# Normalising most of x in a transposed layout, with row statistics spread over the partitions through DRAM

## The reference, cut to what matters

```
hn   = x * rsqrt(mean(x*x, axis=-1) + 1e-6) * norm_g          # per token
proj = hn @ w_in                                              # 9216 columns
q, k, v, z_a, hc, gb, gc, z_b, g = split(proj)
attn = three dilated sliding-window groups, 8 heads of 64, merged by log-sum-exp
a    = (silu(z_a) * attn) @ w_attn_out
u    = gc * hc ;  conv = cw0*u[t-1] + cw1*u[t] + cw2*u[t+1]
c    = (silu(z_b) * gb * conv) @ w_conv_out
y    = rmsnorm(x + (sigmoid(g_a)*a + sigmoid(g_c)*c) @ w_o, final_g)
```

## Time and profile before

| | |
|---|---|
| median of 3 runs | 1518.55 us (1517.28 to 1518.56) |
| the profiled execution | 1517.51 us |
| its span on core 7 | 1515.9 us (cores: 1511.9 to 1515.9) |
| mean granted TensorE clock | 0.997 to 0.999 of full speed on every core |
| busy on core 7 | TensorE 1477.8, VectorE 927.4, ScalarE 697.8, GpSimd 141.5 us |
| moved by DMA | 132.07 MB, mean 87 GB/s |

### The profile page before, as it was taken

How to read it: one execution, slowest core, us unless ns; L and a number is a source line. 1 busy time by engine, 2 the same in 40 slices (tenths; PEclk the granted TensorE clock), 3 DMA queues, 4 the chain that set the end, 5 groups by cost and what they waited for, 6 DMA issues and landing times.

```text
span 1515.9 us, 28477 instructions; the slowest of 8 cores (1511.9 to 1515.9 us)
## 1 busy us (share of the span) xinstructions
PE 1477.8 (97%) x11360; PEld 848.1 (56%) x11360; DVE 927.4 (61%) x1477; ACT 697.8 (46%) x1169; POOL 141.5 (9%) x286
## 2 busy tenths in 40 slices
PE   4999999999999999999999999999999999999997
PEld 2454445577666666666766665766444444444443
DVE  4677777335775848667459575686854444445445
ACT  4445454344565656645356557565322222232222
POOL 4121113000010000100000000001100000000001
PEclk9999999999999999999999999999999999999999
DMA  9965554413150431502424205144943233343233
GB/s 250 153 127 102 117 103 81 72 39 83 32 104 15 100 54 38 82 14 45 106 38 94 40 17 112 27 95 67 188 103 108 83 105 91 84 111 105 62 112 125
DMA packets 67764, 132.07 MB, mean 87 GB/s; under 512 B 8752, under 2 KB 34480, under 8 KB 67376
## 3 DMA queue, kind: packets, MB, share of 16 engines
q1 hardware_dynamic: 49296, 96.70, 24.0%
q0 software_dynamic: 18336, 33.56, 16.5%
HBM read 130.17 MB, written 33.62 MB: 108 GB/s over the span
## 4 chain that ended last, share of the span: by engine, by line
PE 90%; DMA 6%; DVE 3%; issue 1%; ACT 0%; SPq 0%; POOL 0%; DVEq 0%; POOLq 0%; ACTq 0%
PE ps L405 52%; PE ps L699 10%; PE ps L1089 7%; PE ps L1119 6%; PE ps L855 6%; PE ps L719 3%; PE ps L808 3%; DMA X<-xw 2%; DMA gc_s<-X 2%; DMA X<-gc_s 2%; PE ps L450 1%; DVE X L905 1%; DMA v_s<-X 1%; DVE X L830 0%; DVE X L442 0%
## 5 line engine op out<-in xcount | busy, mean ns | idle before, releaser
L405 PE MATMUL ps<-hnT,wbf 128*128 128x512 bf16 (+1 forms) x3008 | 665.5, 373 | 2.6 <-DVE hnT L398 1.6
L405 PEld LDWEIGHTS ps<-hnT,wbf 128*128 128x128 bf16 x3008 | 282.1, 98 | 312.5 <-DVE X L894 2.6
L395 ACT ACTIVATE X<-ps 128x512 bf16<-128x512 f32 (+2 forms) x320 | 219.1, 693 | 201.7 <-PE ps L405 157.7
L820 ACT ACTIVATE X<-ps 128x512 bf16<-128x512 f32 x384 | 204.1, 614 | 116.9 <-PE ps L808 116.9
L405 PE MATMUL ps<-hnT,X 128*128 128x512 bf16 (+1 forms) x1152 | 245.5, 367 | 0.0
L870 DVE TENSOR_TENSOR X<-ps,X 128x512 f32<-128x512 f32 x128 | 110.9, 866 | 157.9 <-PE ps L855 118.5
L405 PEld LDWEIGHTS ps<-hnT,X 128*128 128x128 bf16 x1152 | 108.0, 98 | 125.2
L1094 DVE SCALAR_TENSOR_TENSOR hnT<-hnT,ps 128x512 f32<-128x512 f32 x128 | 87.1, 685 | 146.1 <-PE ps L1089 146.1
L830 DVE TENSOR_TENSOR X<-X,et 128x512 bf16<-128x512 bf16 x384 | 145.9, 419 | 37.3 <-ACT X L820 36.3
L699 PE MATMUL ps<-wbf,hnT 128*128 128x128 bf16 x2720 | 164.6, 220 | 0.0
L699 PEld LDWEIGHTS ps<-wbf,hnT 128*128 128x128 bf16 x2720 | 159.2, 114 | 3.3
(11 more groups left out here) (60 smaller groups left out, 982.4 us busy)
## 6 DMA issues: line engine op xcount, KB each, us to landing
X<-xw SPq DMA_DIRECT2D x80, 512.0 KB, 6.3
wbf<-w_in POOLq DMA_DIRECT2D x95, 256.0 KB, 6.0
y<-X SPq DMA_DIRECT2D x31, 512.0 KB, 3.9
X<-w_in POOLq DMA_DIRECT2D x17, 256.0 KB, 18.9
ga_s<-X SPq DMA_DIRECT2D x32, 128.0 KB, 4.2
X<-ga_s SPq DMA_DIRECT2D x8, 512.0 KB, 8.4
X<-gc_s SPq DMA_DIRECT2D x8, 512.0 KB, 9.1
gc_s<-X SPq DMA_DIRECT2D x24, 128.0 KB, 6.5
```

Source lines behind the costliest of these rows:

```text
L395: return op("act", lambda e: e.activation(out=out, in_=in_, func=AF.Copy), reads=reads, writes=writes)
L405: fns.append(lambda e, kt=kt: e.matmul(bv.cols(c0, n), lhsT=wf(kt), rhs=hnT.cols(kt * WT + t0, n), start=(kt == 0), stop=(kt == 7)))
L820: op("act", lambda e, bv=bank(sb_ + hh), hh=hh: e.activation(out=prv.cols(hh * 512, 512), in_=bv.cols(0, 512), func=AF.Exp, scale=0.125), ...
```

## The change

The host lays x down a second time, as `xt`: per 512 tokens (a group G) four blocks, each with 128 channels on the rows and, in a row, 512 tokens of one channel block and 512 of the next. The first nine tiles are handled as before. The other 39 are handled as ten groups of four tiles (one of three). For a group the kernel still loads its row-wise tiles and takes their squares and scales, but writes the scales as columns of a small tile `rs`, stores these to DRAM (`rs_s`), reads them back so that every partition holds all 512, and lets VectorE multiply the transposed loads by g (now one number per partition) and by those scales, straight into `hnT`. Stages N, T and E are gone for these tiles. `p1_until` now also runs in the middle of each step.

```
+        rs_d = nc.dram_tensor("rs_s", [10, 512], F32)
+        rb_ = [xb(75136 + 2048 * i, 2048, F32) for i in range(2)]
...
-        order = [8, 9, 10, 11, 7] + list(range(12, 41)) + list(range(0, 7)) + list(range(41, 48))
+        order = [8, 9, 10, 11, 7, 12, 13, 14, 15]
...
+        def xa_next():
+            k = xring["i"] % 6
+            xring["i"] += 1
+            return xa[k], "d_xa%d" % k
+
+        def group_events(k, G, nt):
+            t0, n, p = 0.3 + 2.8 * k, 128 * nt, k % 2
+            rb = rb_[p]
+            for t in range(nt):
...
+                def load(t=t, st=st):
+                    st["b"], sname = xa_next()
+                    dma("sp", sname, st["b"].v.base, bass.AP(xw, (512 * G + 128 * t) * D, [[D, 128], [1, D]]),
+                        writes=st["b"].r)
+
+                def square(t=t, st=st):
+                    rms_stat(st["b"].v.base, st["b"].r, xn_[2], out=(rs4.cols(4 * p + t, 1), R_rs4[p]))
+                at = t0 + (0.0, 0.3, 0.9, 1.2)[t]
+                p1ev.append((at, load))
+                p1ev.append((at + 1.0, square))
+
+            def store():
+                dma("sp", "d_rs%d" % p, bass.AP(rs_d, 512 * k, [[nt, 128], [1, nt]]), rs4.cols(4 * p, nt),
+                    reads=[R_rs4[p]], writes=[R_rsd[k]])
+
+            def spread():
+                dma("sp", "d_rb%d" % p, rb.v.cols(0, n), bass.AP(rs_d, 512 * k, [[0, 128], [1, n]]),
+                    reads=[R_rsd[k]], writes=rb.r)
+            p1ev.append((t0 + 2.25, store))
+            p1ev.append((t0 + 2.55, spread))
+            for q in range(4):
...
+                def load(q=q, st=st):
+                    st["b"], sname = xa_next()
+                    dma("sp", sname, st["b"].v.base, bass.AP(xt_d, (4 * G + q) * 128 * 1024, [[1024, 128], [1, 1024]]),
+                        writes=st["b"].r)
+
+                def norm(q=q, st=st):
+                    for j in range(2):
+                        op("dve", lambda e, j=j: e.scalar_tensor_tensor(
+                            out=hnT.ap((2 * q + j) * WT + 512 * G, [[128, nt], [1, 128]]),
+                            in0=st["b"].v.ap(512 * j, [[128, nt], [1, 128]]),
+                            scalar=cf.cols(CF_G + 2 * q + j, 1), in1=rb.v.ap(0, [[1, nt], [nt, 128]]), op0=ALU.mult, op1=ALU.mult),
+                           reads=st["b"].r + rb.r + [R_const], writes=hres(512 * G, 512 * G + n))
+                p1ev.append((t0 + 2.0 + 0.45 * q, load))
+                p1ev.append((t0 + 3.5 + 0.45 * q, norm))
+
+        for k, (G, nt) in enumerate(((4, 4), (5, 4), (6, 4), (7, 4), (8, 4), (9, 4), (10, 4), (1, 3), (0, 4), (11, 4))):
+            group_events(k, G, nt)
+        p1ev.sort(key=lambda x: x[0])
...
-                    conv_step(ct, c)
+                    conv_step(ct, c, mid=lambda: p1_until(stepi + 0.5))
                     stepi += 1
-                    p1_until(21.5 + (stepi - 8) * 1.3)
+                    p1_until(stepi)
                     stores.pop(0)()
```

More of the change, by code:

```diff
@@ L192, in build_program @@
     xw = nc.dram_tensor("xw", [XROWS, D], F32, kind="ExternalInput")
+    xt_d = nc.dram_tensor("xt", [XROWS // 512, 4, 128, 1024], F32, kind="ExternalInput")
     w_in = nc.dram_tensor("w_in", [INW, D], F32, kind="ExternalInput")
@@ L198, in build_program @@
     fgvec = nc.dram_tensor("fgvec", [128, D], F32, kind="ExternalInput")
-    cfp_d = nc.dram_tensor("cfp", [128, 32], F32, kind="ExternalInput")
+    cfp_d = nc.dram_tensor("cfp", [128, 40], F32, kind="ExternalInput")
     cbf_d = nc.dram_tensor("cbf", [128, 256], BF16, kind="ExternalInput")
@@ L223, in build_program @@
         stat_t = sb("stat", [128, 32], F32)
+        rs_t = sb("rs", [128, 8], F32)
         cbf_t = sb("cbfs", [128, 256], BF16)
@@ L228, in build_program @@
         dma_sem_names = (["d_w%d" % i for i in range(NWS)] + ["d_cw%d" % i for i in range(8)]
-                         + ["d_e0", "d_e1", "d_c", "d_c2", "d_gb", "d_fg", "d_wao", "d_wco", "d_g31", "d_vs20", "d_vs21"]
+                         + ["d_e0", "d_e1", "d_c", "d_c2", "d_gb", "d_fg", "d_wao", "d_wco", "d_g31", "d_vs20", "d_vs21", "d_rs0", "d_rs1", "d_rb0", "d_rb1"]
                          + ["d_xa%d" % i for i in range(6)] + ["d_x3%d" % i for i in range(6)] + ["d_y%d" % i for i in range(6)]
@@ L276, in build_program @@
         R_patt = Res()
+        rs4 = View(rs_t[:])
+        R_rs4 = [Res(), Res()]
+        R_rsd = [Res() for _ in range(10)]
         R_gad = [[Res() for _ in range(8)] for _ in range(4)]
@@ L333, in mrg @@
             return hnT.cols(dt_ * WT + m * 512, 512)
-        CF_HB, CF_CW, CF_FL, CF_BG, CF_MH = 0, 16, 28, 32, 48
+        CF_HB, CF_CW, CF_FL, CF_BG, CF_G, CF_MH = 0, 16, 28, 32, 48, 56
         def load_consts():
@@ L341, in load_consts @@
             dma("sp", "d_gb", gb_.v.base, bass.AP(gvec, 0, [[D, 128], [1, D]]), writes=R_gb)
-            dma("sp", "d_c2", cf.cols(CF_CW, 32), cfp_d.ap(), writes=[R_const])
+            dma("sp", "d_c2", cf.cols(CF_CW, 40), cfp_d.ap(), writes=[R_const])
             op("dve", lambda e: e.tensor_scalar(out=cf.cols(CF_HB, 16), in0=cf.cols(CF_BG, 16), scalar1=0.5,
@@ L409, in build_program, with rms_stat @@
         stat_ctr = {"i": 0}
-        def rms_stat(src, src_res, junk=junk_, eng="pool"):
+        def rms_stat(src, src_res, junk=junk_, eng="pool", out=None):
             k = stat_ctr["i"] % 8
@@ L420, in rms_stat @@
                                                  scalar2=EPS, op0=ALU.mult, op1=ALU.add), reads=[r], writes=[r])
-            op(eng, lambda e: e.tensor_tensor(out=stat.cols(c0 + 2, 1), in0=stat.cols(c0 + 1, 1),
-                                                 in1=cf.cols(CF_MH, 1), op=ALU.pow), reads=[r, R_mh], writes=[r])
-            return stat.cols(c0 + 2, 1), r
+            dst, dres = out if out is not None else (stat.cols(c0 + 2, 1), r)
+            op(eng, lambda e: e.tensor_tensor(out=dst, in0=stat.cols(c0 + 1, 1),
+                                                 in1=cf.cols(CF_MH, 1), op=ALU.pow), reads=[r, R_mh], writes=[dres])
+            return dst, dres
         R_gb = gb_.r
@@ L471, in build_program @@
-        p1ev.sort(key=lambda x: x[:3])
+        first = [[fn for (_, _, fn) in p1_stages(i, ti)] for i, ti in enumerate(order)]
+        xring = {"i": len(order)}
+        def xa_next():
[6 more added lines that the diff above has]
+            for t in range(nt):
+                st = {}
+                def load(t=t, st=st):
[16 more added lines that the diff above has]
+            for q in range(4):
+                st = {}
+                def load(q=q, st=st):
[11 more added lines that the diff above has]
+                p1ev.append((t0 + 3.5 + 0.45 * q, norm))
@@ L475, in p1_until @@
             while p1pos["i"] < len(p1ev) and p1ev[p1pos["i"]][0] <= t:
-                p1ev[p1pos["i"]][3]()
+                p1ev[p1pos["i"]][1]()
                 p1pos["i"] += 1
@@ L1299 @@
     cbf = np.ascontiguousarray(np.concatenate([_CACHE["pat"], _CACHE["idn"]], axis=1))
+    gcol = np.asarray(norm_g, np.float32)[0].reshape(8, 128).T
     in_maps = []
@@ L1311 @@
             flags[:, 3] = -1.0
-        cfp = np.ascontiguousarray(np.concatenate([cw, flags, bg], axis=1).astype(np.float32))
-        in_maps.append({"xw": xwin, "w_in": w_in2, "w_ao": w_ao, "w_co": w_co, "w_o": w_o2, "gvec": gvec,
+        cfp = np.ascontiguousarray(np.concatenate([cw, flags, bg, gcol], axis=1).astype(np.float32))
+        xt = np.ascontiguousarray(xwin.reshape(XROWS // 512, 512, 4, 2, 128).transpose(0, 2, 4, 3, 1)).reshape(
+            XROWS // 512, 4, 128, 1024)
+        in_maps.append({"xw": xwin, "xt": xt, "w_in": w_in2, "w_ao": w_ao, "w_co": w_co, "w_o": w_o2, "gvec": gvec,
                         "fgvec": fgvec, "cfp": cfp, "cbf": cbf, "etab": _CACHE["etab"]})
```

## The result

The changed kernel took 1622.65 us in the median of 4 runs (1616.77 to 1628.51), the kernel before 1517.91 us: a ratio of 1.0694, interval [1.0671, 1.0716], 105 us slower. I had forecast slower, by 16 us, with a range up to 1556. The direction was right and the size was not. The profiled execution took 1628.5 us, and its page is of core 6, with a span of 1627.0 us. In some executions of any kernel here the cores of one die show a lower granted clock and take longer; such times are left out, and where a run has no others, the cores of its other die are given.

What follows compares the result with a forecast made beforehand. TensorE, 97% busy, bound the kernel before; a 23 us loop per group would now pace the convolution stage. 70 + 9 x 23 + 11.4 = 288.4 us against 272.1; 1517.5 + 16.3 = 1533.8 us, range 1502 to 1556.

Steps and rivals of the forecast that it cites:

- What goes: Convolution stage: 39 x 0.447 us = 17.4 us of bare TensorE transposes go; ScalarE's copies and VectorE's multiplications weren't on the path.
- The mechanism: Convolution stage: waits from one group's multiplications through loads and scales to the next's form a 23 us loop, exceeding TensorE's 19.35.
- The `gc_s` stores: SyncE's list: they stand behind the spreading and often loads, and line 548 waits; loop taken as 23 us instead of 21.6.
- R: Loop: spreading the scales to every partition, rows 2.3 to 6.1 us, taken as 4 us behind one load.
- S: Loop: storing the scales, from issue to landing, rows 1.5 to 6.7 us, taken as 3 because the queue had emptied.
- L: Loop: landing of a row-wise load, at least 4.0 us, median 6.3; taken as 6.3 us.
- the third rival: Convolution stage: every loop step at its upper median, 27.4 us, giving +56 us, 1573 us; chance 0.10.
- The multiplication: VectorE: each new 128x512 multiplication taken as 0.79 us, between 0.6 and 1.28; eight make 6.3 us a group.
- The clock: Convolution stage: the rows between 100 and 200 us showed a clock of 1.00; no slowdown was put in the sum.
- DMA capacity: DMA engines: 22.6 us of DMA time a group in 19.35 us of TensorE, 21.3 us at best; called the deciding term.
- The start: First transposed group: scales ready near 52 us amid congestion, first multiplications at 70 us where 61 would be on time.
- Rival (a): Convolution stage: transfers keep up, L + S + R stays near 11 us, TensorE paces; 1503 us, chance 0.21.

Runs made afterwards that it cites:

- the run with an eighth of the bytes: Changed kernel, own gc_s resources, four gcs buffers, eight load buffers, later multiplications, scales' DMAs on GpSimd's queue, an eighth of each transposed load: 17 us over the kernel before.
- the list freed: Changed kernel with scales' store and spreading on GpSimd's queue, own gc_s resources, four gcs buffers, eight load buffers, later multiplications: 42 us over the kernel before.
- four edits: Changed kernel with four gcs buffers, eight load buffers, own gc_s resources, scales' DMAs on GpSimd's queue; with multiplications a step later too, 42 us over the kernel before.
- the mixed one: Kernel before with four of ten groups transposed, scales' DMAs on GpSimd's queue, own gc_s resources, scales stored two steps before use: ratio 1.0135.

## Why the prediction was wrong

What goes: right. 312 transposes and ScalarE's 39 copies went, and nothing else in the stage had been on the path.

The mechanism: right in kind. A loop from group to group, longer than TensorE's 19.35 us, paces the stage through VectorE's list and the banks. The step that failed is the one that let the `gc_s` stores run beside this loop instead of in it, and with it several sizes:

- The `gc_s` stores. I named them as pulling the same way and gave them about 1.4 us a loop. They were the longest piece of the chain: 113.0 us in nine loops, 12.6 us each, and VectorE waited 98.4 us for them. The spreading (R), which I had on the path at 4 us, was there for 0.9 us a loop. The run with four `gcs` buffers shows that even so they were not the cause alone: without their wait, R's takes its place, and the distance shrinks by 11 us only.
- S, taken at 3 us, was 5.4 us in the eight times that it lay on the chain (4.2 in the median of the stage). R, taken at 4, was 8.1 in the median. L, taken at 6.3, was 8.0 in the median, but the six loads on the chain took 3.7 to 8.6 us, 35.1 in all, so L didn't lengthen the loop. My argument that the queue would have emptied was wrong: the spreading and the loads go out in one burst behind the wait. With all at the upper medians I had 27.4 us and 1573 us (the third rival), and the kernel went 50 us past that too, since the `gc_s` stores aren't in that sum either.
- Added up, the loop of 32.3 us is 12.6 for `gc_s`, 4.8 for S, 3.9 for L, 0.9 for R (each as its mean over the nine loops) and 10.1 for the rest, where I had 1.4, 3, 6.3, 4 and 8.3.
- The multiplication, taken at 0.79 us because the row had the same length, cost 1.13 us. The run that reads the scales in order (0.73 us) shows that the stride is the difference. The time was 16 us less there, hardly more than one time can tell.
- The clock. I left it at 1.00, from the earlier trace rows. With TensorE standing still for parts of each group it was 0.80 to 0.91: in the one pause that I read closely, from 100 to 110 us of the run with an eighth of the bytes, TensorE was busy 0.06 of 10 us and the granted clock was 0.50, its lower level (1.2 GHz), and 0.83 in the ten microseconds after (columns as above):

```profile
100.00:110.00 10.00, 0.06 (x1) 0.09 (x2) 9.47 (x13) 0.00 (x0) 0.63 (x2) 0.50 0.87 144
110.00:120.00 10.00, 9.78 (x38) 4.16 (x40) 1.82 (x4) 3.38 (x6) 1.18 (x3) 0.83 0.41 95
```

  A projection's matmul of 128x512 took 414 to 419 ns in the mean between 80 and 340 us, where it took 379 before, and the projections of the whole kernel 28.6 us more. How much of that the clock made, and how much of it lay on the path, was not tried by itself.
- DMA capacity, "the term that decides", did not decide: share 0.70 to 0.80 with a loop of 32.3 us is 22.6 to 25.8 us of DMA time a group, where I had 22.6. The sum was a little low, and the loop was longer than it. (It takes the 249 GB/s of the first 30 us for nearly all loads of x; 1.05 of those 7.47 MB went over GpSimd's queue, for the weights, and took 0.22 of the share of 0.94.) With the ring of eight the share reached 0.94 in one stretch, and with the list freed 0.98.

The start (first multiplications at 74.5 us, I had 70) and VectorE's convolution work (4.2 us a step) held.

From the first multiplications (74.5 us) to those of the last group (362.2 us) it is 287.7 us for the 207 of nine loops: 81 us. The start adds 4.5 us. All that stands behind the stage begins 109.6 us later than before (397.67 for 288.12 us), so the end after those multiplications, for which I had 11.4 us, adds the 8 us that are left. That is 93 of the 95 us by which the profiled execution (1628.5 us) exceeds the forecast (1533.8).

Rival (a), the transfers keep up, is refuted by every run. The rule of the Trainium skill by which the loop would have been hidden ("DMA: Bandwidth & Descriptors", "Anatomy of one DMA") was off in the same direction: it gives 2.0 us for 2 KB, where 4.2 us were measured on SyncE's queue and 9.0 us on GpSimd's, and 3.2 us for 512 KB, where 8.0 us were measured. That section fits its rule to DMAs that GpSimd issues; the prediction applied it to SyncE's without saying so.

## What to carry to other kernels

In a list that issues in order, a transfer that waits for a result of this group holds back the loads of the next, and a loop is closed with no buffer in it; draw the loop through the list as well as through the buffers. Two chains of nearly equal length can make a single remedy look useless (four edits that gained 11 us or less each, taken alone, gained 63 us together with the lead): follow each wait that goes to the one that takes its place, and cut them together before calling a cause refuted. And where the bounds of a sum are far apart and several terms come from the same queue, they can err together: don't take values that each need a quiet queue. But no choice within the bounds mends a path that is left out: the medians gave 27.4 us for 32.3 here. Every store whose landing an engine waits for belongs in the sum, at the time that it takes behind the loads in front of it.

## What the runs showed of the hardware

- A VectorE multiplication of 128x512 with a float32 operand read with a stride of four numbers took 1.13 us, with the same operand read in order 0.73 us.
- A store of 2 KB in pieces of 16 B took 4.2 us to land on SyncE's queue in the changed kernel (1.41 us at the least seen in the chain) and 9.0 us on GpSimd's queue in the mixed one; with the queue as the only edit it took 8.6 us.
- The spreading, 256 KB read out of the same 2 KB, took 6.8 us even at a DMA share of 0.52, about as long as a 512 KB load there (6.7 us).
